# A joined two-block transformer kernel: key units in two banks, forget sums in four parts, and modulation rows in rounds of three

## What is computed

```python
# first block
rq, rk, rv, rg, fq, fk, fv, ff = split(rmsnorm(h, g_mix) @ w_in)
ret = silu(rg) * head_group_norm(chunk_retention(rotary(rq), rotary(rk), rv))
fox = forgetting_attention(rmsnorm(fq), rmsnorm(fk), fv, log_sigmoid(ff + b_forget))
h = h + concat([ret, fox]) @ w_out            # 8 heads of 64 each
h = h + memory_cross_attention(rmsnorm(h), mem, w_xq, w_xkv, ...)
h = h + (silu(hn @ w_gate) * (hn @ w_up)) @ w_down
# second block
sh1, sc1, gt1, ..., gt3 = split(silu(c) @ w_ada + b_ada, 9)
x = x + 0.5 * gt1 * swiglu(modulate(rms_norm(x), sh1, sc1), w1_gu, w1_down)
b_g, c_g, u, q, k, v, z_conv, z_attn = split(modulate(rms_norm(x), sh2, sc2) @ w_in)
y_conv = (b_g * short_conv(c_g * u, conv_w)) @ w_conv_proj
y_attn = sliding_window_attention(rope(q), rope(k), v, sinks) @ w_attn_proj
x = x + gt2 * ((sigmoid(z_conv) * y_conv + sigmoid(z_attn) * y_attn) @ w_out)
x = x + 0.5 * gt3 * swiglu(modulate(rms_norm(x), sh3, sc3), w2_gu, w2_down)
return rms_norm(x, g_final)
```

## Time and profile before

| | |
|---|---|
| time, median of 3 runs (range) | 2173.07 us (2171.93 to 2173.85) |
| the profiled execution: time, span | 2173.89 us, 2172.1 us |
| mean granted clock of PE | 0.983 |
| busy: PE, PEld | 2063.7 us (95%), 1684.1 us (78%) |
| busy: DVE, ACT, POOL | 907.5 (42%), 707.4 (33%), 839.8 us (39%) |
| DMA | 233.25 MB, mean 107 GB/s |

### The profile page before, as it was taken

The page is one execution under the profiler, slowest core; times in us unless marked ns, Lnnn a source line. Parts: engine busy times, 40 slices in busy tenths (PEclk is TensorE's granted clock), DMA queues, the critical chain, the costliest instruction groups (busy, mean ns, idle before and its releaser), DMA issues.

```text
span 2172.1 us, 26802 instructions
## 1 busy us (share of the span) xinstructions
PE 2063.7 (95%) x9748; PEld 1684.1 (78%) x9748; DVE 907.5 (42%) x1202; ACT 707.4 (33%) x1065; POOL 839.8 (39%) x347
## 2 busy tenths in 40 slices
PE   7998889989999999999999989998999999999997
PEld 6787678867777778778888878887777877888886
DVE  3576764343788881142221122453443324222112
ACT  4233344234222222232222223223654233222221
POOL 3344223403344444434444433434223443444442
PEclk9999999999999999999999999999999999999999
DMA  5243212303466673223333324422112332333331
GB/s 193 79 137 105 77 44 66 97 20 107 160 233 234 233 250 98 87 78 96 97 97 97 97 87 110 139 90 78 59 59 69 96 99 76 97 97 97 97 97 68
DMA packets 66504, 233.25 MB, mean 107 GB/s; under 512 B 7553, under 2 KB 8833, under 8 KB 65921
## 3 DMA queue, kind: packets, MB, share of 16 engines
q1 hardware_dynamic: 64992, 229.54, 33.1%
q10 hardware_dynamic: 1440, 2.72, 0.4%
HBM read 224.37 MB, written 2.10 MB: 104 GB/s over the span
## 4 chain that ended last, share of the span: by engine, by line
issue 66%; POOL 28%; PE 5%; POOLq 1%; DVE 0%; ACT 0%; DVEq 0%
POOL wlo L403 28%; PE bank L1497 2%; PE bank L1499 2%; PE bank L1498 2%; POOLq L402 0%; POOLq L406 0%; DVE h L1359 0%; DVE ssum L862 0%; POOLq L403 0%; PE bank L1531 0%; PE bank L1521 0%; PE bank L1522 0%; DVE h L943 0%; DVEq L121 0%; ACT tmp L477 0%
## 5 line engine op out<-in xcount | busy, mean ns | idle before, releaser
L403 POOL TENSOR_TENSOR wlo<-raw,whi 128x1024 fp32r<-128x1024 f32 x343 | 839.6, 2449 | 1310.8 <-ACT whi L429 1310.6
L1399 PE MATMUL bank<-xh,whi 128*128 128x512 f32 x1664 | 655.9, 394 | 16.9 <-ACT whi L429 16.0
L1400 PE MATMUL bank<-xl,whi 128*128 128x512 f32 x1664 | 650.5, 391 | 0.0
L429 ACT ACTIVATE whi<-raw 128x1024 fp32r<-128x1024 f32 x343 | 362.3, 1056 | 671.3 <-PE bank L1405 339.2
L1405 PE MATMUL bank<-xh,wlo 128*128 128x512 f32 x1664 | 411.2, 390 | 0.0
L1399 PEld LDWEIGHTS bank<-xh,whi 128*128 128x128 f32 x1664 | 313.5, 188 | 91.0 <-ACT whi L429 17.5
L1400 PEld LDWEIGHTS bank<-xl,whi 128*128 128x128 f32 x1664 | 313.9, 189 | 64.1 <-issue 0.5
L1405 PEld LDWEIGHTS bank<-xh,wlo 128*128 128x128 f32 x1664 | 312.6, 188 | 64.9
L1497 PE MATMUL bank<-hh,whi 128*128 (+1 forms) x528 | 207.2, 392 | 4.9 <-POOL wlo L403 4.7
L1498 PE MATMUL bank<-hl,whi 128*128 (+1 forms) x528 | 206.9, 392 | 0.0
L1499 PE MATMUL bank<-hh,wlo 128*128 (+1 forms) x528 | 206.7, 391 | 0.0
(11 more groups left out here) (258 smaller groups left out, 2064.8 us busy)
## 6 DMA issues: line engine op xcount, KB each, us to landing
raw<-units SPq DMA_DIRECT2D x343, 512.0 KB, 3.5
ada_w<-ada_rows SPq DMA_DIRECT2D x72, 512.0 KB, 4.4
h<-x_t SPq DMA_DIRECT2D x8, 256.0 KB, 6.9
dec<-decays ACTq DMA_DIRECT2D x8, 256.0 KB, 3.0
out_t<-h SPq DMA_DIRECT2D x8, 256.0 KB, 2.1
mem_in<-mem_t SPq DMA_DIRECT2D x1, 1024.0 KB, 12.8
turned_q<-proj SPq DMA_DIRECT2D x4, 256.0 KB, 5.8
turned_k<-proj SPq DMA_DIRECT2D x4, 256.0 KB, 4.1
```

The lines of the kernel that those rows point to most:

```text
L403: pool.tensor_tensor(wlo[:, j % 2 * UNIT:(j % 2 + 1) * UNIT], raw[:, j * UNIT:(j + 1) * UNIT], whi[:, j % 2 * UNIT:(j % 2 + 1) * UNIT].bit ...
L429: act.activation(whi[:, v % 2 * UNIT:(v % 2 + 1) * UNIT], raw[:, slot * UNIT:(slot + 1) * UNIT], ACT.Copy).then_inc(hi_ready, 1)
L1399: mm(bank[:, 0:n], wh, chunk(rhs[0], t, n), start=t == 0, stop=False)
L1400: mm(bank[:, 0:n], wh, chunk(rhs[1], t, n), start=False, stop=False)
```

## The change

- **Modulation rows**: 24 rounds of three rows in place of 12 of six, each row with its own slot. In gu two dots follow the first pair of a turn and one the second; SP loads one row behind each of three units of four. 33 rows are made in gu. Rounds 11 to 17 follow on DVE, then the residual of down's chunks 0 to 3, then rounds 18 to 23, then the sums and the residual of chunks 4 to 7. SP loads three rows behind each of the units 116 to 123 (rows 33 to 56), none behind 124 and 125, and three behind each of 126 to 130.
- **Retention**: key units alternate banks 6 and 7, each after the evacuation of the one two back. The forget sums are in four parts (`forget_log`, `forget_sum`, `forget_split`, `forget_right`), at the end of DVE's steps 0 to 3. `ret_norm_step` is split into functions by kind; mean and variance of pairs 0 and 1 use bank 5, the variance of pairs 2 and 3 bank 6.
- **Fox**: all but the reciprocal of pair 2's late steps, and all of pair 3's, stand on DVE in `beside_exps(hd)`, which `attention` calls between the row maxima of a head and its normalised weights, and on ACT in `retention_rest(hd)`, behind the exponentials. The transposes of `xv` use bank 5. PE no longer takes all banks ahead of fox.
- **cu**: its loop on DVE is written out, and the four turns of the queries stand behind convolutions 4 to 7.
- **Window**: the z_conv unit uses bank 6, after the evacuation of the values of two pairs back; the convolution's unit uses bank 7. The wait for the sigmoid stands ahead of the values.

```diff
-ADA_ROUNDS = 12
+ADA_ROUNDS = 24
...
-                    for n in ((0, 1), (2,), (3, 4), (5,))[j]:
+                    for n in ((0,), (1,), (2,), ())[j]:
                         load_ada(i, n, first)
...
+            half = L["down"].u0 + FC // 2
+            while rows < NMOD * C:
+                load_unit(u, u % 4)
+                u += 1
+                for _ in range(3):
+                    if rows < (57 if u < half + 3 else NMOD * C):
+                        load_ada(rows // ADA_N, rows % ADA_N)
+                        rows += 1
+            while u % 4:
+                load_unit(u, u % 4)
...
+                    if after_exps:
+                        after_exps(hd)
...
+                if hd == 1:
+                    gn_root_of(3)
...
-                                   banks[7][:, M:2 * M].rearrange("p (m n) -> p m n", m=2), ACT.Copy).then_inc(vmem_copied, 1)
-            attention(fox, pair_evac(fox), values_filler)
+                                   banks[5][:, M:2 * M].rearrange("p (m n) -> p m n", m=2), ACT.Copy).then_inc(vmem_copied, 1)
...
+            def retention_rest(hd):
+                if hd == 0:
+                    gn_square(3)
+                    gn_high(2)
+                if hd == 3:
+                    gn_high(3)
+            attention(fox, pair_evac(fox), values_filler, after_exps=retention_rest)
...
-                    act.activation(chunk(tmp, p % 2), banks[7][:, :], ACT.Sigmoid).then_inc(acted, 1)
+                    act.activation(chunk(tmp, p % 2), banks[6][:, :], ACT.Sigmoid).then_inc(acted, 1)
...
+                if js[-1] == C - 1:
+                    norm_chunk(norm, C - 1, dst=dst, gain=gain)
...
-                        extra(i, first, range(0, 3))
+                        extra(i, first, range(0, 2))
...
-                        extra(i, first, range(3, 6))
-                repeat(dve, lay.n // 4, body)
+                        extra(i, first, range(2, 3))
+                if name == "cu":
+                    for i in range(lay.n // 4):
+                        body(i, i == 0)
+                else:
+                    repeat(dve, lay.n // 4, body)
...
+            def forget_log():
...
+            def forget_sum():
...
+            def forget_split():
...
+            def forget_right():
+
+                dve.wait_ge(gate_dve, 5)
...
+            def gn_centre(p):
+
+                ro = chunk(proj, PR["rq"] + p)
+                dve.wait_ge(gn_mean, p + 1)
+                tt(ro, ro, banks[5][:, :], ALU.subtract).then_inc(gn_xc, 1)
...
+            def gn_recip(p):
+
+                dve.wait_ge(gn_root, p + 1)
...
+                dve.reciprocal(chunk(xn, 0), banks[5 if p < 2 else 6][:, :]).then_inc(gn_rstd, 1)
+
+            def gn_scale(p):
+
+                dve.wait_ge(gn_rstd, p + 1)
+                if p >= 1:
+                    dve.wait_ge(gn_y, p)
...
+            def gn_low(p):
+
+                dve.wait_ge(gn_hi, p + 1)
+                tt(chunk(xl, p), chunk(proj, PR["rg"] + p), chunk(xh, p).bitcast(f32), ALU.subtract).then_inc(gn_lo, 1)
...
-                    tt(chunk(kmem, s - 1, M), banks[7][:, 0:M], r_mem[:, :], ALU.mult).then_inc(scaled, 1)
+                    tt(chunk(kmem, s - 1, M), banks[6 + (s - 1) % 2][:, 0:M], r_mem[:, :], ALU.mult).then_inc(scaled, 1)
...
+                if s < 4:
+                    (forget_log, forget_sum, forget_split, forget_right)[s]()
+                if s in (3, 5, 7):
+                    gn_centre((s - 3) // 2)
+                if s in (4, 6, 8):
+                    gn_recip((s - 4) // 2)
+                if s in (4, 6):
+                    gn_scale((s - 4) // 2)
+                if s in (5, 7):
+                    gn_low((s - 5) // 2)
+
+            def beside_exps(hd):
+                if hd == 0:
+                    gn_scale(2)
+                    gn_centre(3)
+                    right_rows(1)
+                if hd == 1:
+                    gn_recip(3)
+                if hd == 2:
+                    gn_scale(3)
+                    gn_low(2)
+                if hd in (3, 5):
+                    dve.wait_ge(fox.s_scores, hd - 1)
                     right_rows((hd + 1) // 2)
+                if hd == 4:
+                    gn_low(3)
 
...
+            attention(fox, None, pair_evac(fox), values_filler, beside_exps)
...
             pairs("gu", (hh, hl), ada_dots)
-            ada_dots(11, False, range(ADA_N))
+
+            def ada_rounds(a, b):
+                with dve.Fori(a, b) as i:
+                    ada_dots(i, False, range(ADA_N))
+            ada_rounds(11, 18)
+            residual("down", "ffn1_2", js=range(0, 4))
+            ada_rounds(18, ADA_ROUNDS)
...
+            residual("down", "ffn1_2", js=range(4, C))
...
+            def later_queries_turn(i, first, js):
+                if i >= 2:
+                    rope(4, turned_qb, qkv, 8, (2 * (i - 2) + (js[0] > 0),))
...
-            rope(4, turned_qb, qkv, 8, range(4))
...
+                if k is not fox:
+                    all_banks_taken()
...
+            def gn_mean_of(p):
+
+                pe.wait_ge(ret_out, p + 1)
+                if p >= 1:
+                    pe.wait_ge(gn_xc, p)
+                if 1 <= p < 3:
+                    pe.wait_ge(gn_rstd, p)
+                mm(banks[5][:, :], mean_head, chunk(proj, PR["rq"] + p), start=True, stop=True).then_inc(gn_mean, 1)
+
...
+            def gn_var_of(p):
+
+                pe.wait_ge(gn_sq, p + 1)
+                if p == 2:
+                    pe.wait_ge(sc, SCALED["xk"] + 7)
+                elif p >= 1:
+                    pe.wait_ge(gn_rstd, p)
+                mm(banks[5 if p < 2 else 6][:, :], mean_head, chunk(tmp, p), start=True, stop=True).then_inc(gn_var, 1)
...
+                    if s < 2:
+                        take(6 + s)
                     if s == 0:
-                        take(7)
                         pe.wait_ge(norm_lo, HI_BASE["mem"] + C)
-                    else:
-                        pe.wait_ge(sc, SCALED["xk"] + s)
+                    elif s >= 2:
+                        pe.wait_ge(sc, SCALED["xk"] + s - 1)
                     u = L["xk"].u0 + s
-                    unit_product(u, u % 2, banks[7], (memh, meml), M)
-            bank_free[7] = [(sc, SCALED["xk"] + C)]
-            bank_free[3] = [(ret_out, 3)]
-            bank_free[4] = [(ret_out, 4)]
-
+                    unit_product(u, u % 2, banks[6 + s % 2], (memh, meml), M)
...
+                    pe.wait_ge(ret_out, 4)
+                pe.wait_ge(vmem_copied, hd + 1)
...
-                    ret_norm_step(NRET + 1)
+                    gn_mean_of(3)
+                if hd == 1:
+                    gn_var_of(3)
+                    pe.wait_ge(gn_xc, 4)
                 if hd >= 1:
+                    if hd >= 2:
+                        pe.wait_ge(fox.s_pt_act, hd - 1)
+                        pe.wait_ge(fox.s_pt_dve, 2 * (hd - 1))
                     pe.wait_ge(sc, SCALED["xv"] + hd)
                     for m in range(2):
-                        last = nc.tensor.transpose(banks[7][:, M + m * P:M + (m + 1) * P],
+                        last = nc.tensor.transpose(banks[5][:, M + m * P:M + (m + 1) * P],
                                                    tmp[:, hd % 2 * T + m * P:hd % 2 * T + (m + 1) * P], ident)
...
+            def unit_part(u, rhs, bank, part):
...
-                    if p == 0:
-                        pe.wait_ge(half_lo, HALVES["b"] + C)
-                    else:
-                        pe.wait_ge(prod, PROD["cz"] + p)
-                    unit_part(L["cz"].u0 + 2 * p, X, 0)
+                    if p >= 2:
+                        pe.wait_ge(swa.s_lo, p - 1)
+                    unit_part(L["cz"].u0 + 2 * p, X, banks[6], 0)
...
-                    pe.wait_ge(acted, ACTED["cz"] + p + 1)
-                    unit_part(L["cz"].u0 + 2 * p + 1, Y, 0)
+                    if p == 0:
+                        pe.wait_ge(half_lo, HALVES["b"] + C)
+                    else:
+                        pe.wait_ge(prod, PROD["cz"] + p)
+                    unit_part(L["cz"].u0 + 2 * p + 1, Y, banks[7], 0)
...
+                    if p < pairs_n:
+                        pe.wait_ge(acted, ACTED["cz"] + p + 1)
                     window_values(p - 1)
                 if p < pairs_n:
-                    unit_part(L["cz"].u0 + 2 * p + 1, Y, 1)
+                    unit_part(L["cz"].u0 + 2 * p + 1, Y, banks[7], 1)
```

144 lines of the change are left out of this document (47 added, 97 removed).

## The result

The changed kernel takes 2134.66 us (median of 4 runs, 2133.61 to 2135.25), against 2172.5 us before, run beside it: a ratio of 0.9825 with an interval of 0.9808 to 0.9842. The forecast was 2134, the range 2117 to 2152. The profiled execution took 2133.61 us, its span is 2131.8, its clock 0.985.

A forecast was written before the change was run, and what follows sets the result against it. PE was taken as the bound nearly everywhere. Terms -19 (retention and forgetting), -13.6 (gu), -6.1 (start of down), +16 (down), -8.9 (cu and b), -7.4 (window) sum to -39.0: 2173.9 to 2134.9, less 0.8: 2134 us; range 2117 to 2152.

The forecast's parts named there:

- Retention and forgetting: Retention through fox's heads: two key banks, spread forget sums and moved norm steps take 19 us off, bounds 13 to 25.
- The clock in fox: From 253.2 to 294.6 us the clock averaged 0.88, so 5.0 us were lost to it.
- Gu: Gu's 41 units: with three dots per round DVE sheds work and PE sets the pace, 13.6 us off, bounds 11 to 15.
- Start of down: Down's start: the 4.57 us wait shrinks to 1.5 and 3.0 of low clock goes, 6.1 off, bounds 3 to 7.6.
- Down: Down: rows 33 to 71 loaded and multiplied beside its units make PE wait, 16 us on, bounds 3 to 30.
- The pace: Down: three rows and a unit load take 7.0 us, against 5.44 of PE per unit.
- (b): Rival: down adds only 4 us, with loads landing in 4 and pace 6; total 2122 us, chance 0.17.
- (c): Rival: fox gives its waits back, DVE bounding heads 0 to 3; total 2142 to 2146 us, chance 0.17.
- (d): Rival: down is dearer, pace 8.5 to 9, costing 30 to 36 us; total 2148 to 2154, chance 0.12.
- (e): Rival: window heads keep their wait through bank 6; total 2141 us, with no chance of its own.
- (f): Rival: slower than before, each down round's three dots meeting GpSimd three times, costing 90 us; total 2208, chance 0.04.
- (g): Rival: the change does nothing to gu, whose pace was never DVE's; total 2147 us, chance 0.02.

The follow-up runs named there:

- burst: The changed kernel with the four forget parts in one burst on DVE at the end of step 1, as before: 2141.1 us.
- one bank: The changed kernel with all key units in bank 7, each behind the evacuation of the one before, forget parts still spread: 2140.6 us.
- norm ahead: The changed kernel with the late group norm steps ahead of the maxima of fox heads 0 to 2, as before: 2141.85 us.
- bank 7: The changed kernel with the transposes of `xv` in the second half of bank 7 again, as before: 2137.2 us.
- half dots: The changed kernel with modulation rows back in 12 rounds of six, and each dot over 512 of 1024 columns only: 2115.22 us.
- six slots: The changed kernel with three more slots for modulation rows from row 39 on, and DVE's loop over the rounds written out: 2121.29 us.

## Why the prediction was right, and where not

**Retention and forgetting (-19, measured -21.1).** The steps came in the forecast places and a little larger. Fox's first scores stand at 242.38 (244.7 forecast), scores of head 1 at 250.50 (253.4), the transposes of head 3 at 275.99 (279.8). The undone parts cost 6.4 (burst), 5.9 (one bank), 7 (norm ahead) and 2.5 (bank 7), 22 in all. Read only between `xk`'s beginning and `xq`'s, in the profiled executions, they cost 7.2, 4.4, 8.6 and 3.4, 23.6 for the 21.1 of the stage. So each is a cause. That they act apart from each other isn't shown: the sum is near the whole, but no run undoes two at once. I had left 1.4 us for one low-clock stretch and it came, behind this wait:

```profile
262.11 0.33 PE L1804 MATMUL bank<-pt_fox,proj 128*64 128x128 f32 x2 [3.04 <-DVE xn L1184]
```

Its size was forecast (2 to 3 us), its reason wasn't: I had `xv`'s evacuation late, but PE's values wait for bank 6, which the moved reciprocal still reads. The wait list showed `pt_fox` at 3.0 in six, where I had let 3.2 in two go; `right_rows` behind the maxima didn't remove them.

**The clock in fox.** The stretch of 41.4 us has 0.96, for 0.88 before: 1.7 us lost, not 5.0. By the Trainium skill, "TensorE: Matmul & The Clock Gate", section "A second HAM failure mode: psum-queue depth-cycling", short idles between groups would have kept the 5.0. This trace has such idles in every head and doesn't agree: the clock fell once, behind the idle of 3.04 us, and not behind those of 0.5 to 1.8. But that it is the length that decides isn't shown either, as the last section says.

**Gu (-13.6, measured -13.3)**, with the cause shown by the half dots. **Start of down (-6.1):** the wait fell from 4.57 to 1.60 and no low clock follows. Before, down took 127.61 us where 22 units of 5.44 are 119.7: 7.9 over. Now the second unit's start costs 1.9 (1.60 idle and the term below): -6.0.

**Down (+16, measured +18.0).** 12.0 + 6.0 = 18.0. Term by term: first half 2.6 forecast, 0.78 + 1.23 + 1.49 = 3.5 measured; middle 7.2 and 7.26; clock behind it 3.0 and 2.7 (13 matmuls at a step of 0.43 in place of 0.23, clock 0.52 in 843.70 to 849.90); behind, 3.2 and 0.36 + 0.26 + 1.61 = 2.2. That makes 15.7. The term that was missing from the forecast: an idle time in the rows is shorter than what it costs. A matmul is shown with 0.39 us and the next starts 0.23 later; the idle is counted from the modelled end of the last one, and the first one after a wait has 0.50. 139.60 us less 119.7 for the units, 14.6 idle and 2.7 of clock leaves 2.6 for eight waits, 0.33 each; seven of them make 2.3, and the sum 18.0. The middle is best seen in SP's queue, with DVE's residual and the dot that released row 57:

```profile
809.66 1.60 SPq L301 DMA_DIRECT2D raw<-units  x3
830.97 2.87 SPq L313 DMA_DIRECT2D ada_w<-ada_rows  x3
833.87 0.44 SPq L301 DMA_DIRECT2D raw<-units  x1
```

```profile
827.32 2.48 DVE L883 TENSOR_TENSOR ssum<-ssum,tmp 128x512 f32<-128x512 f32 x1 [4.06 <-ACT tmp L483]
829.72 1.21 DVE L1040 CUSTOM_DVE_ANT_0 xn<-ada_w,csilu 128x1024 f32<-128x1024 f32 x1
```

The pace was right (7.0 forecast, 7.2 measured) for the wrong reason, and this is the step of the working that failed. 7.0 per three rows came from a stretch of before at 275 GB/s, and I set it beside a time by traffic alone. In that stretch DVE waited for landings three times, 3.7 us, and two of its six dots met a subtraction. With six slots the same bytes go at 6.18 a turn and the DMA engines move up to 411 GB/s: the pace is made of dots that meet subtractions, landings of a ring that is too short, and the start of a loop. By the rule cited from the Trainium skill, "DMA: Bandwidth & Descriptors", section "Specifications", some 358 GB/s, the pace could be 5.9. This case doesn't agree with it as a limit: 411 GB/s over 12.4 us is above it. The average of what was issued, 2.10 MB in 6.18 us or 339 GB/s, is lower; loads issued earlier were still landing (they took 7 to 10 us before 777, and 5 to 7 behind 783).

**Cu and b (-8.9, measured -8.9)** and **window (-7.4, measured -8.4):** eight waits of 0.93 plus the some 0.1 per wait that the idle column leaves out. Bank 6 was free in time, as the spare 2 us had said. The terms' errors (-2.1, +0.3, +0.1, +2.0, 0, -1.0) partly cancel; that the total met the forecast to a microsecond is luck.

Of the rivals, (b), down costs little, is refuted by its waits, (c) by fox's first scores and transposes, which came earlier than forecast, and (d) by a pace of 6.4 to 7.2 in most turns: two of the first half took 8.2 and 8.5. (e) falls with the sigmoid's waits, which are gone. (f) falls too: no turn has three blocked dots. (g) falls with gu's 13.3 us.
